# A two-layer encoder on one core: layers written out, semaphores in two banks, and a rearranged down stage

## The reference

```python
h = rms_norm(x, norm_mlp_pre[l])
f = jnp.square(jax.nn.relu(h @ w_up[l])) @ w_down[l]
x = x + rms_norm(f, norm_mlp_post[l])
```

## Time and profile before

| what | value |
|---|---|
| median of 3 runs | 2977.26 us (2975.03 to 2978.22) |
| the profiled execution's own time | 2972.61 us |
| its span, first to last instruction | 2971.0 us |
| mean granted TensorE clock | 0.957 of 2.4 GHz |
| PE busy | 2721.5 us, 92% of the span |
| DVE busy | 1907.9 us, 64% |
| ACT busy | 1380.2 us, 46% |
| POOL busy | 530.8 us, 18% |
| DMA | 434.75 MB, mean 146 GB/s |
| instructions | 37726, half of them in each layer |

### The profile page before, as it was taken

The page is one execution under the profiler, slowest core; times in us unless marked ns, Lnnn a source line. Parts: engine busy times, 40 slices in busy tenths (PEclk is TensorE's granted clock), DMA queues, the critical chain, the costliest instruction groups (busy, mean ns, idle before and its releaser), DMA issues. The chain is left out here.

```text
span 2971.0 us, 37726 instructions
## 1 busy us (share of the span) xinstructions
PE 2721.5 (92%) x13832; PEld 2275.9 (77%) x13832; DVE 1907.9 (64%) x2780; ACT 1380.2 (46%) x2376; POOL 530.8 (18%) x479
## 2 busy tenths in 40 slices
PE   5998999887979999999879989989878899999997
PEld 4987988666858887788769878867767688877886
DVE  5613866976688876445773157669666888854467
ACT  4312866976443322334433147669643433324344
POOL 2111613970000000000022224349400000000000
PEclk9999999998989999999989999989989899999998
DMA  7243765461224445855433354854322344377554
GB/s 212 62 142 121 227 156 161 67 169 51 79 82 156 147 146 194 268 196 187 157 84 102 129 158 154 227 147 71 109 73 69 107 156 155 132 244 241 190 172 155
DMA packets 333854, 434.75 MB, mean 146 GB/s; under 512 B 86230, under 2 KB 211930, under 8 KB 333404
## 3 DMA queue, kind: packets, MB, share of 16 engines
q1 hardware_dynamic: 333648, 432.23, 48.0%
q10 hardware_dynamic: 12, 0.02, 0.0%
HBM read 289.57 MB, written 140.86 MB: 145 GB/s over the span
## 5 line engine op out<-in xcount | busy, mean ns | idle before, releaser
L2234 PE MATMUL f_ps<-dn_g 128*128 128x512 f32 x2688 | 622.8, 393 | 16.7 <-DVE dn_g L2465 16.7
L2234 PEld LDWEIGHTS f_ps<-dn_g 128*128 128x128 f32 x2688 | 509.4, 190 | 126.1 <-DVE dn_g L2465 14.5
L2465 DVE TENSOR_TENSOR dn_g<-dn_raw,dn_g 128x2048 fp32r<-128x2048 f32 x112 | 256.4, 2291 | 272.1 <-ACT dn_g L2314 272.0
L2224 PE MATMUL f_ps<-hc_h,up_w_h 128*128 128x512 f32 x896 | 352.2, 393 | 26.4 <-DVE up_w_l L2431 20.6
L2314 ACT ACTIVATE dn_g<-dn_raw 128x2048 fp32r<-128x2048 f32 x112 | 214.0, 1914 | 327.4 <-PE f_ps L2234 214.1
L2224 PE MATMUL f_ps<-hc_h,up_w_l 128*128 128x512 f32 x896 | 351.4, 392 | 0.0
L2224 PEld LDWEIGHTS f_ps<-hc_h,up_w_h 128*128 128x128 f32 x896 | 170.2, 190 | 63.9 <-DVE up_w_l L2431 28.0
L2224 PE MATMUL f_ps<-hc_ld,up_w_h 128*128 128x512 f32 x512 | 200.5, 392 | 0.0
L2224 PEld LDWEIGHTS f_ps<-hc_h,up_w_l 128*128 128x128 f32 x896 | 170.1, 190 | 35.4
L510 POOL TENSOR_TENSOR w_row_l<-w_row_first,w_row_h 128x512 fp32r<-128x512 f32 x12 | 15.0, 1275 | 901.3 <-ACT w_row_h L618 901.3
L1316 DVE CUSTOM_DVE_ANT_0 s_ps_c<-s_ps_c,distance 128x1024 f32<-128x1024 f32 x128 | 156.8, 1227 | 14.1 <-PE s_ps_c L1189 14.1
(11 more groups left out here) (309 smaller groups left out, 6393.1 us busy)
## 6 DMA issues: line engine op xcount, KB each, us to landing
act_blocks<-u_stage SPq DMA_DIRECT2D x32, 1792.0 KB, 6.6
dn_raw<-act_blocks SPq DMA_DIRECT2D x112, 512.0 KB, 4.0
mix<-in_w_down SPq DMA_DIRECT2D x128, 256.0 KB, 3.4
down_sums<-mix SPq DMA_DIRECT2D x128, 256.0 KB, 2.8
up_raw<-in_w_up SPq DMA_DIRECT2D x32, 1024.0 KB, 5.3
dn_raw<-down_sums SPq DMA_DIRECT2D x64, 512.0 KB, 5.1
dn_raw<-in_w_down SPq DMA_DIRECT2D x48, 512.0 KB, 4.6
w_raw<-in_w_in SPq DMA_DIRECT2D x16, 512.0 KB, 4.2
```

Source lines behind the costliest of these rows:

```text
L2224: last = nc.tensor.matmul(dst, wt[:, x % RING, k, :], tok, start=(opens[j] and k == 0 and i == 0), stop=(k == KT // 2 - 1 and i == 2), ski ...
L2234: last = nc.tensor.matmul(f_ps[:, bank0[pi] + i, :], lhs[:, n % 4, 0, q, i * P:(i + 1) * P], rhs[:, n % 4, 1, q, :], start=(down_opens[pi] ...
L2465: nc.vector.tensor_tensor(g_l[:, n % 4], dn_raw[:, n % 3], g_h[:, n % 4], ALU.subtract) \
```

## The change

- **Layers written out.** `nc.Fori` becomes a Python `for`: the body is emitted twice, with constant addresses. `final` is true in the second.
- **Semaphores in two banks.** A stage takes its semaphores from one of two banks of 76. `end_stage()` only changes the bank; POOL's list of each stage begins with a clear of the other one. The barrier of `nc.Block` stays. One barrier with a clear stands at the very end of the program. Fifteen of the sixteen barriers of L151 are gone.
- **Last layer.** `pre_square`, `pre_norm`, `turn`, `tok_high`, `tok_low_part` and `first_rows` are left out when `final`.
- **Residual loads.** `residual(t)`, t = 0 to 5, goes behind `load(16 + 4t)`; only the gains stay behind `load(8)`.
- **Near tiles' second norm.** `pre_square` and `pre_norm` of near tile k come one granule later: two granules behind the first norm.

```diff
 class Sems:
     def __init__(self, ctx, nc):
-        handles = [ctx.enter_context(nc.semaphore(n)) for n in SEMS]
-        self.by_name = dict(zip(SEMS, handles))
-        nums = [h.num for h in handles]
-        self.range = range(min(nums), max(nums) + 1)
+        self.banks = [[ctx.enter_context(nc.semaphore(f"event{b}_{i}")) for i in range(BANK)] for b in range(2)]
+        self.now, self.by_name = 0, {}
+
+    def range_of(self, bank):
+        nums = [h.num for h in self.banks[bank]]
+        return range(min(nums), max(nums) + 1)
+
+    def next_stage(self):
+        self.now, self.by_name = 1 - self.now, {}
...
         def end_stage():
-            nc.all_engine_barrier(sems_to_clear=S.range)
+            S.next_stage()
+
+        def clear_last(pool):
+            pool.sem_clear(S.range_of(1 - S.now))
...
+                @block.gpsimd
+                def _(pool):
+                    clear_last(pool)
...
-        with nc.Fori(0, DEPTH) as layer:
+        for layer in range(DEPTH):
+            final = layer == DEPTH - 1
+
             def vec(name, lo=None, hi=None):
-                v = a[name][bass.ds(layer, 1), :]
+                v = a[name][layer:layer + 1, :]
...
                         if t >= HT + 2:
-                            sp.wait_ge(S["hn_done"], t - 1)
+                            if not final:
+                                sp.wait_ge(S["hn_done"], t - 1)
                             sp.wait_ge(S["x_stored"], 16 * (t - 1 - HT))
...
                             sp.wait_ge(x_copied, 16 * NT)
-                            for t in range(HT + 2):
-                                residual(t)
+                        t, r = divmod(n - 2 * NG, 4)
+                        if r == 0 and 0 <= t < HT + 2:
+                            residual(t)
...
-                    first_rows(sp, DEPTH - 1)
+                    if not final:
+                        first_rows(sp, layer + 1)
...
                     def turn(s):
+                        if final:
+                            return
...
                     def pre_square(t):
+                        if final:
+                            return
...
-                        if 1 <= k < HT + 1:
-                            pre_square(k - 1)
+                        if 2 <= k < HT + 2:
+                            pre_square(k - 2)
...
-                        if 1 <= k < HT + 1:
-                            pre_norm(k - 1)
+                        if 2 <= k < HT + 2:
+                            pre_norm(k - 2)
...
             end_stage()
+        nc.all_engine_barrier(sems_to_clear=S.range_of(1 - S.now))
```

More of the change, by code:

```diff
@@ L16 @@
 from contextlib import ExitStack
+import itertools
 import math
@@ L91, in shape_constants @@
     return {k: np.ascontiguousarray(v, dtype=np.float32) for k, v in tables.items()}
[L94 to L105, removed]
+BANK = 76
 class Sems:
     def __init__(self, ctx, nc):
-        handles = [ctx.enter_context(nc.semaphore(n)) for n in SEMS]
-        self.by_name = dict(zip(SEMS, handles))
-        nums = [h.num for h in handles]
-        self.range = range(min(nums), max(nums) + 1)
+        self.banks = [[ctx.enter_context(nc.semaphore(f"event{b}_{i}")) for i in range(BANK)] for b in range(2)]
[5 more added lines that the diff above has]
+        self.now, self.by_name = 1 - self.now, {}
     def __getitem__(self, name):
+        if name not in self.by_name:
+            self.by_name[name] = self.banks[self.now][len(self.by_name)]
         return self.by_name[name]
@@ L142, in build @@
         rel_copied = ctx.enter_context(nc.semaphore("rel_copied"))
+        names = itertools.count()
         def sb(c, name, shape, dt=F32):
@@ L147, in ps @@
         def ps(c, name, shape, dt=F32):
-            return c.enter_context(nc.psum_tensor(name, shape, dt))
+            return c.enter_context(nc.psum_tensor(f"{name}{next(names)}", shape, dt))
         def end_stage():
-            nc.all_engine_barrier(sems_to_clear=S.range)
+            S.next_stage()
+        def clear_last(pool):
+            pool.sem_clear(S.range_of(1 - S.now))
         ident = sb(ctx, "ident", [P, P])
@@ L962, in _ @@
                         fetch(sp)
-                if pool_work is not None:
-                    @block.gpsimd
-                    def _(pool):
+                @block.gpsimd
+                def _(pool):
+                    clear_last(pool)
+                    if pool_work is not None:
                         pool_work(pool)
@@ L2201, in _ @@
                     sp.wait_ge(S["near_stored"], 32 * HT)
-                    sp.wait_ge(S["row_landed0"], 16 * ROWS_FIRST)
+                    if not final:
+                        sp.wait_ge(S["row_landed0"], 16 * ROWS_FIRST)
                 @block.tensor
```

2 lines of the change are left out of this document (added).

## The result

| | before | after |
|---|---|---|
| median, same chip | 2976.77 us (2975.03 to 2978.22, 4 runs) | 2909.27 us (2906.62 to 2911.34, 4 runs) |
| profiled execution, its span | 2972.6, 2971.0 us | 2908.1, 2906.4 us |
| mean granted clock | 0.957 | 0.968 |
| PE busy | 2721.5 us | 2696.7 us |

The ratio is 0.9773 [0.9756, 0.979]: 67.5 us less by the medians, 64.6 by the spans. The forecast was 60.4 less. On another chip the same kernel gave 0.9767 [0.9752, 0.9781].

The account below looks back on a forecast made before the run. PE bounds the kernel (busy 2721.5 of 2971.0 us) and the change can only close its holes: 16.5 + 4.1 + 11.8 + 8.6 + 19.4 = 60.4 us, median 2977.3 to 2917 us, range 2907 to 2934.

Parts of the forecast that it names:

- barriers and loop: Stage ends and loop: fifteen second barriers of 1.1 us go, 16.5 us, and the back edge, 4.1 us.
- residual loads: Down part, behind the block of residual loads: PE holes of 4.17 and 3.99 us and 1.8 us half clock each, 11.8 us.
- second norm, both layers: Near tiles: the hole at `turn(0)` and its half clock go, 8.6 us a layer, twice 17.2.
- last layer without next norm, beyond the lag: Second layer's end: 19.4 us go, of which the hole at `turn(0)` is 8.6; 10.8 left.
- rival E: Stage starts: shorter holes also spare PE half clock, 1.8 us each at 5 of them; 2908, chance 5%.
- rival B: Down part: the residuals stall the ring in a new place, up to 11.8 us back; 2929, chance 7%.
- The walk: First layer's near tiles, stepped through with trace durations: third sum ready at 1441.5, 1.7 us before `turn(0)` needs it.
- rival A: First layer's near tiles: final sums still late, `turn(0)` waits, up to 8.6 us back; 2925.5, chance 9%.
- Second layer's end: From granule 49's end to the span's end: 63.2 us become 43.8, so 19.4 us go.
- the one microsecond of slack for the last residual: Second layer's end: residuals 6 and 7 ready 8.7 us behind the store's issue, wanted about 9.7 behind it.
- Rival D: Written-out code stalls in instruction fetch, 4.1 us a stall, 15 on PE's path decide; 24 give 3015; chance 3%.
- Rival C: Stage ends: barriers don't give their price, engines wait at the remaining barrier or for the same DMAs; 2933.5, chance 6%.

Follow-up runs that it names:

- x2: Kernel after, but residual loads in one block behind `load(8)`, second norm one granule behind, last layer's norm kept; 2944.66 us, ratio 0.9904.
- x3: Kernel before with the residual loads spread and nothing else; 2961.36 us, ratio 0.9952.
- x4: Kernel before with the near tiles' second norm two granules behind, in both layers, and nothing else; 2957.34 us, ratio 0.9941.
- y3: Kernel after with the last layer's next norm put back; 2917.81 us, ratio 0.9807.
- x1: Kernel before with its layers written out, PSUM tile names numbered, and nothing else; 2971.49 us, ratio 0.9994.
- y2: Kernel after with a second barrier at each stage end that clears the bank, in place of the clear in POOL's list; 2921.66 us, ratio 0.9826.
- y4: Kernel after with the near tiles' second norm one granule behind, as before; 2916.63 us, ratio 0.9809.
- z0: Kernel after run again unchanged, as the level for the third set; 2904.64 us, ratio 0.9767.
- y1: Kernel after with a second barrier, bare of any clear, put back at each stage end; 2915.01 us, ratio 0.9804.
- z1: Kernel after with products that nobody reads in PE's holes around stage c's start; 2901.65 us, ratio 0.9758.

## Why the prediction was right, and where its sum was off

The time, 2909.3, lies in the range (2907 to 2934), below the likeliest 2917 by 7.7 us. By its own steps:

| term | forecast | by medians | by ratio | from |
|---|---|---|---|---|
| barriers and loop | 20.6 | 28.2 | 28.6 | x2 |
| residual loads | 11.8 | 11.5 | 14.3 | x3 |
| second norm, both layers | 17.2 | 15.5 | 17.6 | x4 |
| last layer without next norm, beyond the lag | 10.8 | 8.5 | 10.1 | y3 |
| sum | 60.4 | 63.7 | 70.6 | the change: 67.5 |

- **Barriers.** The time of each was right (1.40 to 0.30 us at a boundary, forecast 1.1), and the clear at the head of POOL's list cost nothing. The failing step is "Fifteen go: 15 x 1.1 = 16.5 us": it priced an idle stretch at its length alone. Where the clock stood was in the trace (0.56 and 0.52 in the windows above) and I had read it only behind the residual holes. I had the case as rival E, with 5 places at 1.8 us, 2908, and a chance of 5%. That was too little for what happened: four stages, 2.8, 2.2, 1.7 and 1.8 us shorter beyond the barrier (and the second layer's stage d by 2.3, the first layer's not). So the measured time is E's outcome more than the forecast's. That E's amount fitted is partly luck: its 1.8 us were read behind a hole of the down part, from eight products that PE ran without a pause, and in stage c PE waits for ACT and DVE between its products. Which places it picks was not foreseen by anything I read.
- **The loop.** 4.1 us at its place, as forecast; alone it doesn't show in the time (x1).
- **Residual loads.** Right in both reasons, and in size within the interval: the holes went and no new one came, so rival B fell. But the hole is no fixed price: over the kernels that keep the block of residual loads it was 4.08 to 5.99 us in the first layer and 1.33 to 5.09 in the second. The holes at the start of the down part, before any residual is loaded, grew from 2.92 to 4.53 us in the first layer and from 3.30 to 4.95 in the second; I had no term for that. It is not the residuals: x1, which changes only the loop, shows 4.21 and 4.61. Nor is it the loop alone: x3 keeps the loop and has 2.86 and 4.91, and y2, written out, has 3.04 in its first layer. The cause stays open.
- **Near tiles.** The walk held to 0.2 us, and rival A fell with it. In size the term is 7.6 to 8.1 us by y4's stage length against the other kernels', 6.4 against after's own, where I said 8.6.
- **Second layer's end.** 43.8 us, forecast 43.8, the one microsecond of slack for the last residual excepted. The whole feed-forward stage is 22.8 us shorter in after and 24.6 in z0, the same kernel, where the terms gave 25.2; the new holes at the down part's start, named above, take 1.6 us of after's gain.
- **Rival D** fell with x1: straight code of twice the length shows no stall in stages b and c. The Trainium skill, Runtime: NRT & Kernel Launch, section Instruction fetch mechanics, says that the streaming of straight code is mostly hidden and that a taken branch out of the fetched window stalls on a fetch of its target. The trace agrees on both (1.40 us at the written-out boundary, 5.52 at the loop's, with 3.70 in TensorE's branch); that these 3.70 us are a fetch no run here shows.
- **Rival C** fell in a way that I hadn't written: barriers gave more than their price.

Only the barrier term is off by more than its interval, 7.6 us too small; the others lie within 3 us of their forecast by either reading. A miss of 0.26% of the time is small, but it is a miss of 11% of the gain. That the time fell inside the range owes something to E having been taken into it.

## What to carry to other kernels

A barrier costs its own time at every boundary and, where PE ran at half clock for longer behind it, more than that: 1.8 us on top of 0.33 in y1's stage c. Price a hole on PE by its length and by the granted clock in the window behind it, and read that clock at every boundary. In two engines with hand-ordered lists, a step that waits for the other engine's work of the same step is worth moving one step back, and here walking it through with durations of the trace held to 0.2 us over seven steps. Take each part of a change by itself before trusting a sum: here the sum was near and one term was 7.6 us off. And when products are added to raise the clock, read the clock in the window afterwards: in stage c it rose, at two other places it did not.

## What the runs showed that I had not expected

- With a bare barrier of 0.33 us at every boundary both stages c were 2.2 us longer than in after (y1), and with 22 products of ident by ident in the holes around its start 2.1 and 3.8 us shorter (z1). The Trainium skill, TensorE: Matmul & The Clock Gate, section HAM oscillation, puts the price of half clock at half of its duration. The runs here show less: stage c lost 1.8 us between a window of 20.5 us at 0.67 and one at 0.50, that is, for about 7 us more at 1.2 GHz, a quarter; an estimate from two windows. In z0's timeline PE stands for ACT's `first_c` again and again in this window, up to 1.77 us at a time. That part of the slower products falls into time that PE would have waited is the likely reason; it was not tried.
- One binary (z0) shows stage c at 137.7 and at 135.9 us in the two layers of one execution, with the same hole of 1.12 us before its first product. From one profile a single stage can't be compared to better than 2 us.
- The second barrier costs 0.33 us bare, 0.8 with a clear of 76 semaphores and 1.1 with the clear of all 130; the difference is the clear (0.44 and 0.74 us), on the path of all engines.
